# The experts' weights start 32 bytes further on in slots longer by 64 bytes, and one row tile is folded into another

## The chip, the cores and the metric

The kernel runs on one core of a Trainium2 chip. The metric is the device time of one execution, in microseconds (us). A time of the kernel is the median of several executions; the profile shows one execution on its own.

## The reference

Two model blocks are computed one after the other on x of 256 tokens by 1024 features, all in fp32. The first block has two layers of mLSTM and retention heads. The second has two layers of a mixer (a convolution beside banded attention), the first layer followed by a dense SwiGLU, the second by a mixture of eight experts of which each token uses two:

```
logits = t @ w_router + b_router
top_val, top_idx = lax.top_k(logits, 2)
combine = sum(one_hot(top_idx, 8) * softmax(top_val)[..., None], axis=1)
for e in range(8):
    out = out + combine[:, e:e + 1] * ((silu(t @ w_gate[e]) * (t @ w_up[e])) @ w_down[e])
```

Each expert has w_gate and w_up of 1024 x 3584 and w_down of 3584 x 1024. Every layer's shift, scale and gate come from a modulation `silu(c) @ w_ada[l] + b_ada[l]`.

## The kernel before

**Units.** All large weights stream once from HBM through one path, in units of 1 MB (128 partitions x 2048 fp32). SP's queue loads a unit into a slot of `raw` (`load`, L507). ScalarE casts it to the first part, `whi` (`high`, L707), VectorE subtracts to get the second part, `wlo = raw - whi` (`low`, L1738), and TensorE multiplies with both. A product of fp32 accuracy is made from three matmuls in TensorE's fp32r type: first part by first part, second by first, first by second. `whi` and `wlo` have HL = 3 slots of UW = 2048 elements (8192 bytes) in each partition; `raw` has 3 slots for weights before the experts and 6 in the experts. Semaphores tie the slots: SP waits for VectorE to have read a `raw` slot (raw_free), ScalarE and VectorE wait for TensorE to have used a `whi`/`wlo` slot (unit_done), TensorE waits for raw_free.

**The experts.** There are eight jobs of 42 units, 336 in all. 28 units hold columns of w_gate and w_up; for each of four row blocks in a unit there are three matmuls (L1641 to L1643) with a stationary operand of 128 x 128 tokens from `xghi` or `xglo`, and 512 columns of `whi` or `wlo` as the moving operand. 14 units hold rows of w_down; there `thi` and `tlo` are stationary (L1670 to L1672), and 512 columns of `whi` or `wlo` move again. That is 12 matmuls a unit. Between units there are short stretches of other matmuls: transposes (L1627), the spreading of a finished job (L1616), the gathering of tokens for the next (L1608).

**Before the experts** the weights are mostly the stationary operand, and 256 tokens of `hhi`, `hlo`, `yhi` or `ylo` move (L1127 to L1129, L1182 to L1184); for values they move, 256 columns at a time (L1168 to L1170). The gate products of the first block (L1336 to L1338) have `ghi` and `glo` as stationary operand, a narrow one of GROUP + H = 36 columns: slice d of these tiles starts 144·d bytes behind the tile's start, and there are eight slices with three matmuls each.

**Addresses.** Tiles lie one behind the other in the order in which they are allocated. In the built program `whi` starts at byte 65,664 of each partition, `wlo` at 90,240, `hhi` at 131,200, `thi` at 164,480, `xghi` at 201,344, `ghi` at 223,936 and `glo` at 225,088: all multiples of 64. All slots and all operands of 128 or more columns taken from them start at multiples of 64 as well.

**The modulation.** VectorE sums the products of `w_ada` units with the silu of c into `acc` and `acc2`, two running sums (`ada`, L1782 to L1797). In each mixer ScalarE copies a finished row from PSUM into `arow` (L1003), TensorE turns it into columns (L1541), and VectorE takes the columns.

Of the kernel before, what the change touches and what calls it, by code (L numbers as in the profile page):

```python
# [5 lines left out]
F32 = mybir.dt.float32  # L6
F32R = mybir.dt.float32r
I32 = mybir.dt.int32
ACT = mybir.ActivationFunctionType
ALU = mybir.AluOpType  # L10
AX = mybir.AxisListType

P = 128
S = 256
D = 1024
KD = D // P
# [22 lines left out]
FE = 3584  # L39
# [19 lines left out]

UW = 2048
RAW = 6
HALF = 3
MOE_SLOTS = (3, 4, 5, 2, 0, 1)
HL = 3
# [31 lines left out]
S_MOE = S_B3 + UNIT_L2  # L97
# [155 lines left out]
def two_block_model(nc, x, positions, consts, c, w_ada, b_ada, norm_g, w_in, conv_w, conv_b, b_igate, b_fgate,  # L253
# [7 lines left out]
    with ctx:  # L261
        def sb(name, shape, dt=F32, stack=ctx):
            return stack.enter_context(nc.sbuf_tensor(name, shape, dt))
# [3 lines left out]

        raw = sb("raw", [P, RAW, UW])
        whi = sb("whi", [P, HL, UW], F32R)  # L270
        wlo = sb("wlo", [P, HL, UW], F32R)
        xT = sb("xT", [P, KD, S])
        h = sb("h", [P, KD, S])
        hhi = sb("hhi", [P, KD, S], F32R)
# [17 lines left out]
        acc2 = sb("acc2", [P, S])  # L292
# [61 lines left out]
        b2 = ExitStack()  # L354
# [13 lines left out]
        st2 = sb("st2", [P, 2, 8], F32, b2)  # L368
        mean512 = sb("mean512", [P, P], F32, b2)
        cpad = sb("cpad", [P, KD, 2 * GROUP - 1], F32, b2)  # L370
        arow = sb("arow", [P, S], F32, b2)
        b2.close()

# [9 lines left out]
        thi = sb("thi", [P, FE // P, P], F32R, bm)  # L384
        tlo = sb("tlo", [P, FE // P, P], F32R, bm)
        htok = sb("htok", [P, 2, D], F32, bm)
        xghi = sb("xghi", [P, KD, 2, P], F32R, bm)
        xglo = sb("xglo", [P, KD, 2, P], F32R, bm)
# [40 lines left out]
        raw_free = sem("raw_free")  # L429
        hi_ready = sem("hi_ready")  # L430
# [269 lines left out]
        def _(act):  # L700
            step = Chain(act, scalar_step)

            def high(u):
                act.wait_ge(raw_in[u.raw], u.loads)
                if u.n >= HL or u.per:
                    act.wait_ge(unit_done, u.done(1 - HL))
                nc.scalar.copy(whi[:, u.hl, :], raw[:, u.raw, :]).then_inc(hi_ready, 1)  # L707

            def inverse_root(to, of, ready, value, least=eps, loaded=False):

# [51 lines left out]
            for l in range(L):  # L762
                for at, v in ((P1_BADA, b_ada[l]), (P1_NORM, norm_g[l]), (P1_CB, conv_b[l]), (P1_GNM, gn_m[l]), (P1_GNR, gn_r[l])):
                    k = v.shape[0] // P
# [44 lines left out]
            for l in range(L):  # L809
# [11 lines left out]
                for h_no in range(H):  # L821
                    hd = Head(l, h_no)
                    q, k, v, o, z, rq, rk, rv, rz = hd.units
# [197 lines left out]
            for j in range(FF_UNITS):  # L1021
                u, i = Unit(S_FF + j), j // 2
# [82 lines left out]
        def _(pe):  # L1105
            mm = nc.tensor.matmul
# [113 lines left out]
            for k in range(KD):  # L1220
                for t in range(2):
                    last = nc.tensor.transpose(ps2[k // 2][:, k % 2, t * P:(t + 1) * P], xtok[:, t, k * P:(k + 1) * P], ident)
# [4 lines left out]
            for i in range(L):  # L1227
                last = nc.tensor.transpose(ps4[4][:, i], prow[:, i, :], ident)
# [70 lines left out]
            for l in range(L):  # L1299
                if l:  # L1300
                    norm(l)
                for h_no in range(H):
                    hd = Head(l, h_no)
                    q, k, v, o, z, rq, rk, rv, rz = hd.units
# [27 lines left out]
                    else:  # L1332
                        pe.wait_ge(glo_ready, 2 * l + 2)
                        sums = ps2[6][0:GROUP + H, 0]
                        for d in range(KD):
                            mm(sums, ghi[:, d], hhi[:, d], start=d == 0, stop=False)  # L1336
                            mm(sums, ghi[:, d], hlo[:, d], start=False, stop=False)
                            last = mm(sums, glo[:, d], hhi[:, d], start=False, stop=d == KD - 1)  # L1338
# [4 lines left out]
                    if h_no == 0:  # L1343
                        pe.wait_ge(a_ready, l + 1)
                        for t in range(2):
                            last = mm(ps[5][:, t * H:(t + 1) * H], g_a[:, t * P:(t + 1) * P], ident[0:H, 0:H], start=True, stop=True)
# [22 lines left out]
                    if hd.n == 0:  # L1369
                        pe.wait_ge(rows_in, ROWS_LOADED)  # L1370
                        for i, rows in enumerate(P2_ROWS + (CW * CT, CW * CT)):
                            last = nc.tensor.transpose(ps4[6][:, i, 0:rows], prow[0:rows, L + i, :], ident[0:rows, 0:rows])
# [194 lines left out]
            for k in range(KD):  # L1567
# [3 lines left out]
                last = mm(ps[7][g:g + NE, 0:S], wr[:, k], h[:, k], start=k < 4, stop=k >= 4, skip_group_check=True)  # L1571
            last.then_inc(logits_done, 1)
            for i in range(4):
                for k in range(4 * (i % 2), 4 * (i % 2) + 4):
                    last = nc.tensor.transpose(ps[i][:, P * (k % 4):P * (k % 4) + P], h[:, k, i // 2 * P:(i // 2 + 1) * P], ident)
                last.then_inc(htok_done, 1)
                if i == 0:
                    pe.wait_ge(lrow_ready, 1)
                    for t in range(2):
                        last = mm(ps[7][:, S + t * NE:S + (t + 1) * NE], lrow[:, t * P:(t + 1) * P], sel[:, 0:NE], start=True, stop=True)  # L1580
# [38 lines left out]
            def expert(job, mine, x, following):  # L1619
                chunks = JOB_UP // 4  # L1620

                def turn(c):
                    pe.wait_ge(ma_ready, job.count(chunks, c + 1))
                    if c:
                        pe.wait_ge(tlo_ready, job.count(chunks, c))
                    for i in range(4):
                        last = nc.tensor.transpose(ps4[4][:, i], ma[:, c % 2, i * P:(i + 1) * P], ident)  # L1627
                    last.then_inc(turned, 1)

                for i in range(JOB_UP):  # L1630
                    u, c, kind, half = job.unit(i), i // 4, i % 4 // 2, i % 2
                    if c >= 2 and half == 0:
                        pe.wait_ge((mg_ready, ma_ready)[kind], job.count(chunks, c - 1))
                    if i < 2:
                        pe.wait_ge(xghi_ready, mine.whole(i))
                        pe.wait_ge(xglo_ready, mine.whole(i))
                    pe.wait_ge(raw_free, u.free())
                    o = ps[2 * kind + c % 2][:, :]
                    for kk in range(4):
                        k, w = 4 * half + kk, slice(512 * kk, 512 * kk + 512)  # L1640
                        mm(o, xghi[:, k, x], whi[:, u.hl, w], start=k == 0, stop=False)  # L1641
                        mm(o, xglo[:, k, x], whi[:, u.hl, w], start=False, stop=False)  # L1642
                        last = mm(o, xghi[:, k, x], wlo[:, u.hl, w], start=False, stop=k == KD - 1)  # L1643
                    last.then_inc(unit_done, 1)
                    if c and i % 4 == 1:
                        turn(c - 1)
                    if i % 4 == 3 and 1 <= c <= 4 and 1 <= job.n < NE:

                        if c == 1:
                            pe.wait_ge(yexp_ready, job.count(2, 0))  # L1650
                            pe.wait_ge(pickT_ready, job.count(1, 0))
                        else:
                            pe.wait_ge(spread_taken, job.count(4, c - 5))
                        spread(job, c - 1, ps2[7])
                    if i == 4 * 5 + 3:
                        if 1 <= job.n < NE:
                            pe.wait_ge(spread_taken, job.count(4, 0))
                        pe.wait_ge(pickw_ready, mine.count())
                        for t in range(2):
                            last = nc.tensor.transpose(ps[7][:, t * P:(t + 1) * P], pickw[:, t, x], ident)  # L1660
                        last.then_inc(pickT_done, 1)
                for d in range(JOB_DOWN):
                    u = job.unit(JOB_UP + d)
                    pe.wait_ge(tlo_ready, job.count(chunks, d // 2 + 1))
                    pe.wait_ge(raw_free, u.free())
                    for i in range(2):
                        f = 2 * d + i
                        for n in range(2):
                            o, w = ps[5 + n][:, :], slice(D * i + 512 * n, D * i + 512 * n + 512)
                            mm(o, thi[:, f], whi[:, u.hl, w], start=f == 0, stop=False)  # L1670
                            mm(o, tlo[:, f], whi[:, u.hl, w], start=False, stop=False)  # L1671
                            last = mm(o, thi[:, f], wlo[:, u.hl, w], start=False, stop=f == FE // P - 1)  # L1672
                    last.then_inc(unit_done, 1)
                    if d == 0:
                        turn(chunks - 1)
                    if following is not None and d % 3 == 1 and d < 12:
                        if d == 1:
                            pe.wait_ge(pick_ready, following.count())
                            pe.wait_ge(hthi_ready, 2)
                            pe.wait_ge(pickT_ready, job.count(1, 1))  # L1680
                        gather_pair(following, d // 3)
# [44 lines left out]
        def _(dve):  # L1726
            step = Chain(dve, vector_step)
            V = nc.vector
# [5 lines left out]
            def low(u):  # L1734
                dve.wait_ge(hi_ready, u.count())
                if u.n >= HL or u.per:
                    dve.wait_ge(unit_done, u.done(1 - HL))
                V.tensor_tensor(wlo[:, u.hl, :], raw[:, u.raw, :], whi[:, u.hl, :].bitcast(F32), ALU.subtract).then_inc(raw_free, 1)  # L1738

            def norm_tile(n, k):  # L1740
                V.scalar_tensor_tensor(h[:, k], xT[:, k], amul[:, n, k:k + 1], rstd[:], ALU.mult, ALU.mult).then_inc(t_ready, 1)
# [123 lines left out]
            for l in range(L):  # L1865

                last = V.tensor_scalar(par1[:, l, P1_GNM:P1_GNM + KD], par1[:, l, P1_GNM:P1_GNM + KD], 0.5, None, ALU.mult)
# [99 lines left out]
            for l in range(L):  # L1967
# [5 lines left out]
                for h_no in range(H):  # L1973
                    hd = Head(l, h_no)
                    q, k, v, o, z, rq, rk, rv, rz = hd.units
# [17 lines left out]
                    for tap in range(CONV_K):  # L1993
                        if h_no == 0 and tap == 2:
                            gates_summed(l)
                        for x in range(2):
                            for t in range(2):
                                w = column(l, h_no, P1_CW + tap * 2 * KD + x * KD, t)
                                src = qpad[:, x, t, tap:tap + S]
                                if tap == 0:  # L2000
                                    last = V.tensor_scalar(qacc[:, x, t], src, w, column(l, h_no, P1_CB + x * KD, t), ALU.mult, ALU.add)
                                else:
                                    step.wait(back=3)
                                    last = V.scalar_tensor_tensor(qacc[:, x, t], src, w, qacc[:, x, t], ALU.mult, ALU.add)
# [53 lines left out]
                    for o_, t in ((slice(0, S), S), (slice(S, S + P), P)):  # L2058
                        last = V.scalar_tensor_tensor(sT[:, o_], ps[2][:, o_], HD ** -0.5,
                                                      cst[:, h_no * S + C_DECAY:h_no * S + C_DECAY + t], ALU.mult, ALU.mult)  # L2060
# [209 lines left out]
            for j in range(FF_UNITS):  # L2270
                u, i = Unit(S_FF + j), j // 2
# [244 lines left out]
```

## Time and profile before

| | |
|---|---|
| median of 3 runs | 2150.38 us (2146.89 to 2151.61) |
| the profiled execution | 2151.25 us, of which 2149.4 us from the first to the last instruction |
| TensorE busy | 2096.3 us (98%) |
| VectorE busy | 1753.4 us (82%) |
| ScalarE busy | 1321.3 us (61%) |
| moved by DMA | 595.07 MB, mean 277 GB/s |
| the stretch of the experts | about 1150 to 2135 us of the span |

TensorE's busy time counts a matmul from its start to its modelled end, and the ends of matmuls lie behind the starts of the next ones. So how fast TensorE goes is read from the distance between starts in the timeline, not from the length of one matmul.

### The profile page before, as it was taken

The numbers are of one execution on the slowest core, as the hardware profiler recorded it, in microseconds if no ns is written. First come the engines' busy times: TensorE is split into PE (matmuls) and PEld (weight loads), VectorE is DVE, ScalarE is ACT, GpSimd is POOL, SyncE is SP. The second block draws the span as 40 slices with busy tenths as digits, with TensorE's granted clock in tenths as the row PEclk, the third lists the DMA queues.
The fourth block names the chain that finished last, engine by engine and source line by source line (L and its number), as shares of the span: only waits on it lengthen the run. The fifth ranks groups of instructions, "written<-read, shape, count | busy, mean of one in ns | idle before, by whom it ended". The sixth has DMA issues, their size and how long they took to land.

```text
span 2149.4 us, 33810 instructions
## 1 busy us (share of the span) xinstructions
PE 2096.3 (98%) x13585; PEld 1866.9 (87%) x13585; DVE 1753.4 (82%) x2161; ACT 1321.3 (61%) x1265; POOL 30.9 (1%) x60
## 2 busy tenths in 40 slices
PE   7999999999999999999999999999999999999998
PEld 5899999899999889999987888888888888888887
DVE  3978875877767878887877988888888888889887
ACT  3565554566645753434656777777777677776775
POOL 3000000000000000000000000000000000000000
PEclk8999999999999999999998999999999999999999
DMA  9777855666656548987545999999999999999995
GB/s 318 239 218 226 247 188 163 198 191 213 184 189 223 189 138 281 288 303 265 177 170 205 369 353 347 374 358 343 361 350 380 345 345 357 362 366 344 360 348 197
DMA packets 356161, 595.07 MB, mean 277 GB/s; under 512 B 10376, under 2 KB 201368, under 8 KB 356008
## 3 DMA queue, kind: packets, MB, share of 16 engines
q1 hardware_dynamic: 352864, 586.92, 79.1%
q0 software_dynamic: 2752, 5.86, 1.2%
q8 instruction: 110, 1.80, 0.3%
q14 instruction: 43, 0.35, 0.0%
q10 hardware_dynamic: 392, 0.13, 0.0%
HBM read 591.80 MB, written 4.22 MB: 277 GB/s over the span
## 4 chain that ended last, share of the span: by engine, by line
PE 82%; DVE 8%; DMA 3%; ACT 3%; issue 3%; SPq 0%; POOL 0%; DVEq 0%; POOLq 0%
PE ps L1641 9%; PE ps L1643 9%; PE ps L1642 9%; PE ps L1127 5%; PE ps L1128 5%; PE ps L1129 5%; PE ps L1670 5%; PE ps L1671 5%; PE ps L1672 5%; PE ps L1182 3%; PE ps L1183 3%; PE ps L1184 3%; DVE acc L1794 2%; DVE wlo L1738 2%; ACT whi L707 1%
## 5 line engine op out<-in xcount | busy, mean ns | idle before, releaser
L1738 DVE TENSOR_TENSOR wlo<-raw,whi 128x2048 fp32r<-128x2048 f32 x485 | 1109.0, 2288 | 264.9 <-ACT whi L707 249.5
L707 ACT CAST whi<-raw 128x2048 fp32r<-128x2048 f32 x485 | 926.0, 1909 | 389.0 <-PE ps L1643 133.7
L1127 PE MATMUL ps<-hhi,whi 128*128 128x256 f32 x1360 | 393.4, 289 | 0.2
L1128 PE MATMUL ps<-hlo,whi 128*128 128x256 f32 x1360 | 385.9, 284 | 0.0
L1129 PE MATMUL ps<-hhi,wlo 128*128 128x256 f32 x1360 | 385.8, 284 | 0.0
L1641 PE MATMUL ps<-whi,xghi 128*128 128x512 f32 x896 | 360.4, 402 | 0.8 <-DVE wlo L1738 0.8
L1643 PE MATMUL ps<-wlo,xghi 128*128 128x512 f32 x896 | 350.1, 391 | 0.0
L1642 PE MATMUL ps<-whi,xglo 128*128 128x512 f32 x896 | 349.0, 390 | 0.0
L1127 PEld LDWEIGHTS ps<-hhi,whi 128*128 128x128 f32 x1360 | 262.1, 193 | 7.3 <-issue 7.0
L1128 PEld LDWEIGHTS ps<-hlo,whi 128*128 128x128 f32 x1360 | 262.1, 193 | 0.3
L1129 PEld LDWEIGHTS ps<-hhi,wlo 128*128 128x128 f32 x1360 | 261.9, 193 | 0.0
L1643 PEld LDWEIGHTS ps<-wlo,xghi 128*128 128x128 f32 x896 | 168.2, 188 | 36.7
L1641 PEld LDWEIGHTS ps<-whi,xghi 128*128 128x128 f32 x896 | 168.3, 188 | 34.2 <-DVE wlo L1738 1.2
L1642 PEld LDWEIGHTS ps<-whi,xglo 128*128 128x128 f32 x896 | 168.6, 188 | 33.7
L1670 PE MATMUL ps<-whi,thi 128*128 128x512 f32 x448 | 175.3, 391 | 0.0
L1671 PE MATMUL ps<-whi,tlo 128*128 128x512 f32 x448 | 174.5, 390 | 0.0
L1672 PE MATMUL ps<-wlo,thi 128*128 128x512 f32 x448 | 174.4, 389 | 0.0
L1794 DVE SCALAR_TENSOR_TENSOR acc<-raw,cact,acc 128x256 f32<-128x256 f32 x324 | 132.7, 478 | 0.0
L1672 PEld LDWEIGHTS ps<-wlo,thi 128*128 128x128 f32 x448 | 84.1, 188 | 17.7
L1670 PEld LDWEIGHTS ps<-whi,thi 128*128 128x128 f32 x448 | 84.2, 188 | 16.8
L1671 PEld LDWEIGHTS ps<-whi,tlo 128*128 128x128 f32 x448 | 84.2, 188 | 16.6
L1168 PE MATMUL ps<-whi,hhi 128*128 128x256 f32 x320 | 92.3, 289 | 0.0
(398 smaller groups left out, 3029.8 us busy)
## 6 DMA issues: line engine op xcount, KB each, us to landing
raw<-in_moe_w_gate_dram SPq DMA_DIRECT2D x112, 1024.0 KB, 6.1
raw<-in_moe_w_up_dram SPq DMA_DIRECT2D x112, 1024.0 KB, 6.1
raw<-in_moe_w_down_dram SPq DMA_DIRECT2D x112, 1024.0 KB, 5.0
raw<-in_w_in_dram SPq DMA_DIRECT2D x92, 1024.0 KB, 5.6
raw<-in_w_ada_dram SPq DMA_DIRECT2D x69, 1024.0 KB, 7.8
raw<-in_w_out_dram SPq DMA_DIRECT2D x24, 1024.0 KB, 5.0
raw<-in_ffn_w_gate_dram SPq DMA_DIRECT2D x11, 1024.0 KB, 9.1
raw<-in_ffn_w_up_dram SPq DMA_DIRECT2D x11, 1024.0 KB, 8.3
```

The source lines that it names most:

```text
L707: nc.scalar.copy(whi[:, u.hl, :], raw[:, u.raw, :]).then_inc(hi_ready, 1)
L1127: mm(ps2[u.bank][:, j], whi[:, u.hl, w], hhi[:, k], start=k == 0, stop=False)
L1128: mm(ps2[u.bank][:, j], whi[:, u.hl, w], hlo[:, k], start=False, stop=False)
L1129: last = mm(ps2[u.bank][:, j], wlo[:, u.hl, w], hhi[:, k], start=False, stop=k == KD - 1)
L1641: mm(o, xghi[:, k, x], whi[:, u.hl, w], start=k == 0, stop=False)
L1642: mm(o, xglo[:, k, x], whi[:, u.hl, w], start=False, stop=False)
L1643: last = mm(o, xghi[:, k, x], wlo[:, u.hl, w], start=False, stop=k == KD - 1)
L1670: mm(o, thi[:, f], whi[:, u.hl, w], start=f == 0, stop=False)
L1671: mm(o, tlo[:, f], whi[:, u.hl, w], start=False, stop=False)
L1672: last = mm(o, thi[:, f], wlo[:, u.hl, w], start=False, stop=f == FE // P - 1)
L1738: V.tensor_tensor(wlo[:, u.hl, :], raw[:, u.raw, :], whi[:, u.hl, :].bitcast(F32), ALU.subtract).then_inc(raw_free, 1)
L1794: last = V.scalar_tensor_tensor(sums[k % 2], w[:, k], cact[:, block, k:k + 1], sums[k % 2], ALU.mult, ALU.add)
```

## The change

The two tiles of the parts are allocated with 16 more elements (64 bytes) in each slot, under new names. `whi` and `wlo` become views of their first 2048 elements, `ehi` and `elo` views that start 8 elements (32 bytes) further on. Units of the experts (`u.n >= S_MOE`) are cast into `ehi`, subtracted into `elo` and multiplied from there; all other units use `whi` and `wlo`. `arow` is no longer a tile of its own but another name of `acc2`.

```
+HALF_LINE = 8
...
-        whi = sb("whi", [P, HL, UW], F32R)
-        wlo = sb("wlo", [P, HL, UW], F32R)
+        wide_hi = sb("wide_hi", [P, HL, UW + 2 * HALF_LINE], F32R)
+        wide_lo = sb("wide_lo", [P, HL, UW + 2 * HALF_LINE], F32R)
+
+        whi, wlo = wide_hi[:, :, 0:UW], wide_lo[:, :, 0:UW]
+        ehi, elo = wide_hi[:, :, HALF_LINE:UW + HALF_LINE], wide_lo[:, :, HALF_LINE:UW + HALF_LINE]
...
-        arow = sb("arow", [P, S], F32, b2)
+        arow = acc2
...
-                nc.scalar.copy(whi[:, u.hl, :], raw[:, u.raw, :]).then_inc(hi_ready, 1)
+                nc.scalar.copy((whi if u.n < S_MOE else ehi)[:, u.hl, :], raw[:, u.raw, :]).then_inc(hi_ready, 1)
...
-                        mm(o, xghi[:, k, x], whi[:, u.hl, w], start=k == 0, stop=False)
-                        mm(o, xglo[:, k, x], whi[:, u.hl, w], start=False, stop=False)
-                        last = mm(o, xghi[:, k, x], wlo[:, u.hl, w], start=False, stop=k == KD - 1)
+                        mm(o, xghi[:, k, x], ehi[:, u.hl, w], start=k == 0, stop=False)
+                        mm(o, xglo[:, k, x], ehi[:, u.hl, w], start=False, stop=False)
+                        last = mm(o, xghi[:, k, x], elo[:, u.hl, w], start=False, stop=k == KD - 1)
...
-                            mm(o, thi[:, f], whi[:, u.hl, w], start=f == 0, stop=False)
-                            mm(o, tlo[:, f], whi[:, u.hl, w], start=False, stop=False)
-                            last = mm(o, thi[:, f], wlo[:, u.hl, w], start=False, stop=f == FE // P - 1)
+                            mm(o, thi[:, f], ehi[:, u.hl, w], start=f == 0, stop=False)
+                            mm(o, tlo[:, f], ehi[:, u.hl, w], start=False, stop=False)
+                            last = mm(o, thi[:, f], elo[:, u.hl, w], start=False, stop=f == FE // P - 1)
...
-                V.tensor_tensor(wlo[:, u.hl, :], raw[:, u.raw, :], whi[:, u.hl, :].bitcast(F32), ALU.subtract).then_inc(raw_free, 1)
+                hi, lo = (whi, wlo) if u.n < S_MOE else (ehi, elo)
+                V.tensor_tensor(lo[:, u.hl, :], raw[:, u.raw, :], hi[:, u.hl, :].bitcast(F32), ALU.subtract).then_inc(raw_free, 1)
```

No engine gets another instruction, another order or another wait. What changes are addresses. The tiles behind the two parts start 384 bytes (six slots of 64) further on: `hhi` at 131,584, `thi` at 164,864, `xghi` at 201,728, still multiples of 64. `wide_hi` starts at 65,664 and `wide_lo` at 90,432. The slots of `ehi` start at 65,696, 73,952 and 82,208, and those of `elo` at 90,464, 98,720 and 106,976: each is 32 bytes past a multiple of 64, and so is each moving operand of the experts' matmuls, while their stationary operands remain at multiples of 64.

## Rows read from the trace of the kernel before

**Rows 1.** The page: busy time of the engines, and TensorE's granted clock in 40 slices

```profile
PE 2096.3 (98%) x13585; PEld 1866.9 (87%) x13585; DVE 1753.4 (82%) x2161; ACT 1321.3 (61%) x1265; POOL 30.9 (1%) x60
...
PEclk8999999999999999999998999999999999999999
```

**Rows 2.** Windows: busy time of each engine, clock, DMA share and GB/s, experts

```profile
1150.00:2135.00 985.00, 982.81 (x4501) 813.91 (x4500) 860.85 (x542) 708.30 (x477) 0.00 (x0) 1.00 0.97 350
```

**Rows 3.** Lines L1642 and L1671: count, duration in ns (min/median/max), first and last start

```profile
L1642 PE MATMUL ps<-whi,xglo x896: 387/389/402, 1149.2 to 2097.8; 128*128 128x512 f32 x180
```
```profile
L1671 PE MATMUL ps<-whi,tlo x448: 387/389/398, 1229.6 to 2136.4; 128*128 128x512 f32 x150
```

**Rows 4.** Timeline of TensorE (start us, length us), in a unit of w_down

```profile
1504.13 0.39 PE L1670 MATMUL ps<-whi,thi 128*128 128x512 f32 x1
...
1506.17 0.39 PE L1670 MATMUL ps<-whi,thi 128*128 128x512 f32 x1
```

**Rows 5.** Timeline of TensorE, 24 matmuls of 256 columns apart

```profile
539.93 0.28 PE L1127 MATMUL ps<-hhi,whi 128*128 128x256 f32 x1
...
542.82 0.28 PE L1127 MATMUL ps<-hhi,whi 128*128 128x256 f32 x1
```

**Rows 6.** The chain, in order of time: four plain fp32 matmuls of 256 columns

```profile
1307.15 0.86 PE ps L1616 x4
```

**Rows 7.** Timeline of TensorE: gate products, first matmul of each slice, then L1168

```profile
53.98 0.28 PE L1336 MATMUL ps<-hhi,ghi 128*36 128x256 f32 x1
...
54.33 0.28 PE L1336 MATMUL ps<-hhi,ghi 128*36 128x256 f32 x1
...
54.69 0.28 PE L1336 MATMUL ps<-hhi,ghi 128*36 128x256 f32 x1
...
55.03 0.28 PE L1336 MATMUL ps<-hhi,ghi 128*36 128x256 f32 x1
...
55.39 0.28 PE L1336 MATMUL ps<-hhi,ghi 128*36 128x256 f32 x1
...
55.74 0.28 PE L1336 MATMUL ps<-hhi,ghi 128*36 128x256 f32 x1
...
56.09 0.28 PE L1336 MATMUL ps<-hhi,ghi 128*36 128x256 f32 x1
...
56.43 0.28 PE L1336 MATMUL ps<-hhi,ghi 128*36 128x256 f32 x1
...
56.77 0.28 PE L1168 MATMUL ps<-whi,hhi 128*128 128x256 f32 x1
```

**Rows 8.** Timeline of TensorE, units of w_gate behind a spreading (L1616)

```profile
1417.37 0.40 PE L1642 MATMUL ps<-whi,xglo 128*128 128x512 f32 x1
...
1419.22 0.39 PE L1641 MATMUL ps<-whi,xghi 128*128 128x512 f32 x1
...
1422.40 0.39 PE L1643 MATMUL ps<-wlo,xghi 128*128 128x512 f32 x1
```

**Rows 9.** Groups by line, 1300 to 2100 us: busy us, mean ns, idle before

```profile
L1738 DVE TENSOR_TENSOR wlo<-raw,whi 128x2048 fp32r<-128x2048 f32 x271 | 620.0, 2289 | 102.5 <-ACT whi L707 102.4
L707 ACT CAST whi<-raw 128x2048 fp32r<-128x2048 f32 x272 | 520.4, 1913 | 191.4 <-PE ps L1643 116.1 <-PE ps L1672 75.2
```

**Rows 10.** Waits of SP's queue, 1300 to 2100 us: us in total, times, longest

```profile
SPq L507 <- DVE wlo L1738: 638.8, 270, 3.2
```

**Rows 11.** DMA: rate from 1113 to 1130 us, then 1300 to 2100, then landings there

```profile
DMA packets 3195, 6.35 MB, mean 374 GB/s; under 512 B 108, under 2 KB 108, under 8 KB 3193
```
```profile
DMA packets 119871, 284.49 MB, mean 356 GB/s; under 512 B 4336, under 2 KB 4336, under 8 KB 119830
```
```profile
DMA to landing us min/median/max: 4.7/5.7/8.2
```

**Rows 12.** Tile arow: ScalarE's copy into it

```profile
L1003 ACT COPY arow<-ps x2: 372/372/373, 774.0 to 1108.4; 128x256 f32<-128x256 f32 x2
```

## Prediction

> **What bounds the kernel now.** The page comes first: TensorE is busy 98% of the span and its granted clock is full but for the start and the change of stage before the experts [rows 1]. Next the windows: in the 985 us of the experts TensorE is busy 982.81 us at a clock of 1.00, VectorE 860.85, ScalarE 708.30 [rows 2]. A busy TensorE may still be badly fed, so the third view is the waits. ScalarE's cast waits for TensorE to give a slot back, VectorE's subtraction waits for the cast [rows 9], and SP waits 638.8 us in 270 loads for a `raw` slot [rows 10]. Everybody waits backwards towards TensorE, so in this stretch its pace is the time. The DMA engines look full (share 0.97), but moved 350 GB/s [rows 2], against a mean of 374 GB/s over a stretch at 1113 us where several loads stood in the queue, its quiet last microsecond included [rows 11].
>
> The change moves exactly one thing that this could hang on: the place of the moving operand against a 64-byte grid, with the stationary operand left on the grid.
>
> **The change part by part.** The experts have 896 + 448 matmuls for each of three lines [rows 3], 3 x 1344 = 4032. At 0.2267 us that is 914 of the 985 us, and each nanosecond by which the distance changes is worth 4.03 us.
>
> What does 32 bytes do to the distance? No row shows a moving operand off the grid in fp32r. The nearest rows are the gate products, whose stationary operand walks over it: slice d starts 144·d bytes on, that is 0, 16, 32, 48, 0, 16, 32 and 48 bytes past a multiple of 64, under the same moving operands on the grid. The slices of three matmuls take 0.35, 0.36, 0.34, 0.36, 0.35, 0.35, 0.34 and 0.34 us [rows 7]. So 0.117 us each over the first six, and 0.113 over the last six matmuls, at 32 and 48 bytes. Against 0.1067 that is a surcharge of 6.7 ns, half of the usual one. These rows say that the surcharge is no constant, and that the two slices at 32 bytes are among the shortest; they don't prove the address, for slice 3 at 48 bytes took 0.36, the matmuls have only 36 stationary columns, and the pattern also settles with time. Such settling is seen elsewhere: behind a spreading eight matmuls take 1.85 us, 0.231 each, and the next fourteen 3.18 us, 0.227 each [rows 8]. So two streams, the moving one and the load of the next weights, fall into step with each other, and where each starts on the grid may set that step.
>
> Bounds. Best: the surcharge falls to the plain type's 1.7 ns; 11.7 ns x 4032 = 47 us less. Worst: every matmul keeps the distance of the unsettled ones, 0.231, or 4.6 ns more, +19 us; or it needs one 64-byte block more, 33 where there were 32, 16 columns at 2.4 GHz = 6.7 ns, +27 us. Between ends that far apart I take the nearest row, the 0.113 us of the slices at 32 and 48 bytes: the surcharge halves, 6.7 ns less a matmul, **6.7 x 4032 = 27 us less**.
>
> Does the rest keep pace? A unit falls from 985/336 = 2.93 us by 12 x 6.7 = 80 ns to 2.85. A unit is 1.0486 MB, so the loads need 368 GB/s, under the 374 of the loaded queue and with landings of 5.7 us, two units' time, in front of six slots [rows 11]. VectorE has 861 us of work for 958 us [rows 2], its subtraction is 2.289 us, the cast 1.913 [rows 9]. All this hides still; the cover is thin for the loads (at the best case of 2.79 us they need 376 GB/s, and a few us come back).
>
> The cast and the subtraction now write 32 bytes off the grid, and the subtraction reads one operand so. Between nothing and the whole slack: VectorE's idle time, 124 us over 336 units, is 0.37 us a unit, or 0.29 after the gain. I take nothing, since ScalarE and VectorE would have to lose a tenth of their rate before TensorE waited.
>
> `arow` as `acc2`: the same copy of 0.372 us, twice [rows 12]. It waits for the last sum as before, and VectorE's next sum stands behind its own wait for the turned row. Nothing, on either side of one copy (0.7 us in all). The 384 bytes by which the other tiles move leave the grid as it was; a grid of 128 bytes would be changed for the 256-column matmuls, since slots of 8256 bytes start alternately at 0 and 64 on it. Some seven thousand of them at 1 ns would be 7 us, of either sign; I take nothing.
>
> Sum: 2151.25 - 27 = **2124 us**. The profiled execution lies 0.9 us above the median of 2150.38, so against the median the same step gives 2123.5.
>
> The Trainium skill speaks against this sum. "TensorE: Matmul & The Clock Gate", section "Step-by-step: what each phase is for", gives the engine two independent read ports and says that loading the next weights takes no bandwidth from the running matmul. By that no address matters and the sum is 0. The same page's "Back-to-back issue gap" has 518 cycles for 512 columns; the trace's 0.2267 us are 544 cycles, so this case has a surcharge that the page doesn't know. "SBUF — State Buffer", section "Specifications (TRN2)", has lines of 16 bytes: 32 bytes are two whole lines, which again would change nothing.
>
> **The rivals.**
>
> 1. No effect. The surcharge could be a matter of time alone: it is 13.4 and 13.7 ns for operands of both widths, and the settling of [rows 8] happens with all addresses alike modulo 64. For it: slice 3. Against it: identical matmuls one after another settle within nine, the gate slices wander over eighteen. Time 2150.
> 2. Slower. If the moving stream is fetched in blocks of 64 bytes, 2048 bytes that begin half-way touch 33 blocks, and each matmul holds the stream for one block more: 6.7 ns, +27 us, 2178 us. It needs no conflict with the weights' load, only a fetch in rigid slots. It decides once the additional block costs more than the step regained: from +1.1 ns a matmul it is measurable. Against it: the gate slices at 32 and 48 bytes, which also straddle blocks, are on the mean no longer than those on the grid.
> 3. The surcharge vanishes: 2104 us, perhaps 2108 with the loads short of time.
> 4. A gain in a part only, since on a grid of 128 bytes the slots stand at 32 and 96 in turn: 1 to 5 ns on the mean, 2131 to 2147 us.
> 5. VectorE becomes the bound because of its shifted operands. It takes 13% more on its 2.289 us; nothing in the profile hints at it.
>
> **How the numbers follow.** The surcharge halves 0.38; vanishes 0.13; a part only 0.07: faster by more than 0.2% (about what a measurement of this kernel can tell from no change) 0.58. No effect 0.18. Slower 0.24: the additional block 0.19, rival 5 and the other tiles' 128-byte places 0.05. The likeliest case's own range is 2116 to 2132 (2 ns a matmul either way). The whole range goes from 2100, below case 3, to 2170, which takes in the unsettled distance of case 2 (2151 + 19) and leaves out its full block; that leaves out less than two tenths.
>
> **What the changed profile would show.** Right: in the timeline nine settled matmuls of the experts in 1.98 us in place of 2.04, the stretch of the experts about 958 us long, the 256-column matmuls before it still at 0.120, TensorE still without idle time, ScalarE's waits for TensorE shorter by some 80 ns a unit, DMA in the experts near 360 GB/s. No effect: 2.04 us again. The additional block: 2.10 us. VectorE as bound: a subtraction over 2.5 us, and TensorE idle behind L1738 (in the new numbering). The forecast is wrong if the step is set by time and not by address, or if the shift costs a block.

## The result

| | median | runs |
|---|---|---|
| before | 2149.58 us | 10 (2146.74 to 2151.81) |
| changed | 2156.93 us | 10 (2153.62 to 2160.83) |

The ratio is 1.0036, with a 95% interval of 1.0025 to 1.0046: the change makes the kernel slower by 0.36%. I had forecast 1.2% faster. The profiled execution took 2154.86 us, 2.1 us below its median, with a span of 2153.0 us; it is 3.6 us longer in its span than the profile before, and the comparison below accounts for these 3.6.

The page of the changed kernel, as in [rows 1]:

```profile
PE 2098.2 (97%) x13585; PEld 1850.4 (86%) x13585; DVE 1754.1 (81%) x2161; ACT 1318.9 (61%) x1265; POOL 31.0 (1%) x60
...
PEclk8999999999999999999999999999999999999999
```

The windows of the experts' stretch, as in [rows 2] (which had 985 us):

```profile
1134.00:2140.00 1006.00, 1004.61 (x4516) 816.96 (x4515) 863.11 (x544) 706.71 (x478) 0.00 (x0) 1.00 0.96 343
```

The experts' lines, as in [rows 3]. Every line has moved by 4 or 5 numbers:

```profile
L1646 PE MATMUL ps<-wide_hi,xglo x896: 389/393/403, 1134.7 to 2100.6; 128*128 128x512 f32 x180
```
```profile
L1675 PE MATMUL ps<-wide_hi,tlo x448: 389/393/403, 1216.6 to 2140.1; 128*128 128x512 f32 x150
```

From the first start of the one to the last of the other it is 1005.4 us, where [rows 3] give 2136.4 - 1149.2 = 987.2: the experts lost **18.2 us**. But their first matmul starts at 1134.7 instead of 1149.2: all that comes before them gained **14.5 us**. The sum is +3.7, the difference of the spans. Two effects of opposite sign, each more than three times the 0.2% (4.3 us) that the measurement can tell apart, nearly cancel.

Both are in the distance between starts. TensorE's timeline in a unit of w_down, two starts with 24 matmuls between them, then one of 256 columns before the experts, again 24 apart:

```profile
1375.70 0.39 PE L1674 MATMUL ps<-wide_hi,thi 128*128 128x512 f32 x1
...
1381.28 0.39 PE L1674 MATMUL ps<-wide_hi,thi 128*128 128x512 f32 x1
```
```profile
521.85 0.28 PE L1131 MATMUL ps<-hhi,wide_hi 128*128 128x256 f32 x1
...
524.67 0.28 PE L1131 MATMUL ps<-hhi,wide_hi 128*128 128x256 f32 x1
```

5.58 us for 24 is 0.2325 us, against 0.2267 in [rows 4]. 2.82 us for 24 is 0.1175, against 0.1204 in [rows 5].

The other engines have the same work as in [rows 9] and wait for TensorE a little longer, and SP's wait is that of [rows 10]:

```profile
L1743 DVE TENSOR_TENSOR wide_lo<-raw,wide_hi 128x2048 fp32r<-128x2048 f32 x266 | 608.9, 2290 | 115.0 <-ACT wide_hi L711 114.5
L711 ACT CAST wide_hi<-raw 128x2048 fp32r<-128x2048 f32 x267 | 508.7, 1905 | 200.1 <-PE ps L1647 119.4 <-PE ps L1676 80.7
```
```profile
SPq L511 <- DVE wide_lo L1743: 640.8, 265, 3.2
```

A subtraction takes 2.290 us (2.289 before), a cast 1.905 (1.913): places 32 bytes off the grid cost ScalarE and VectorE nothing.

In what follows, a job's mean distance is worked out from the starts of its 504 matmuls in the trace, those before which or behind which something else ran left out, as are the few stops of over 0.26 us. Before, it is 0.2277 to 0.2280 in the eight jobs; in the changed kernel 0.2326 to 0.2327. For the 256-column fp32r matmuls with the weights before the experts (7152, of which some 6900 have their like on both sides), it is 0.1199 before and 0.1176 changed. The short rows in fences show a stretch of 24, mostly settled, and can lie a nanosecond off their job's mean.

### The profile page after: what moved, and what is told of

Same layout as the page of the kernel before. It is cut to its first block, busy times and chain, and to the rows that moved or that the text cites. A ratio compares the mean times of both kernels' runs of the same rounds, so it can differ in the third digit from the quotient of the medians.

```text
span 2153.0 us, 33810 instructions
## 1 busy us (share of the span) xinstructions
PE 2098.2 (97%) x13585; PEld 1850.4 (86%) x13585; DVE 1754.1 (81%) x2161; ACT 1318.9 (61%) x1265; POOL 31.0 (1%) x60
## 4 chain that ended last, share of the span: by engine, by line
PE 85%; DVE 7%; issue 3%; ACT 3%; DMA 2%; SPq 0%; POOL 0%; DVEq 0%; POOLq 0%
PE ps L1647 9%; PE ps L1646 9%; PE ps L1645 9%; PE ps L1131 5%; PE ps L1132 5%; PE ps L1133 5%; PE ps L1676 5%; PE ps L1675 5%; PE ps L1674 5%; PE ps L1186 3%; PE ps L1187 3%; PE ps L1188 3%; DVE wide_lo L1743 1%; DVE acc L1799 1%; PE ps L1620 1%
## 5 line engine op out<-in xcount | busy, mean ns | idle before, releaser
L1743 DVE TENSOR_TENSOR wide_lo<-raw,wide_hi 128x2048 fp32r<-128x2048 f32 x485 | 1109.5, 2289 | 274.5 <-ACT wide_hi L711 257.9
L711 ACT CAST wide_hi<-raw 128x2048 fp32r<-128x2048 f32 x485 | 923.4, 1904 | 396.7 <-PE ps L1647 142.4
L1131 PE MATMUL ps<-hhi,wide_hi 128*128 128x256 f32 x1360 | 388.5, 286 | 0.4 <-DVE wide_lo L1743 0.4
L1132 PE MATMUL ps<-hlo,wide_hi 128*128 128x256 f32 x1360 | 380.5, 280 | 0.0
L1133 PE MATMUL ps<-hhi,wide_lo 128*128 128x256 f32 x1360 | 380.3, 280 | 0.0
L1645 PE MATMUL ps<-wide_hi,xghi 128*128 128x512 f32 x896 | 363.2, 405 | 0.6 <-DVE wide_lo L1743 0.6
L1647 PE MATMUL ps<-wide_lo,xghi 128*128 128x512 f32 x896 | 354.4, 395 | 0.0
L1646 PE MATMUL ps<-wide_hi,xglo 128*128 128x512 f32 x896 | 353.9, 395 | 0.0
L1131 PEld LDWEIGHTS ps<-hhi,wide_hi 128*128 128x128 f32 x1360 | 255.8, 188 | 7.4 <-issue 7.1
L1132 PEld LDWEIGHTS ps<-hlo,wide_hi 128*128 128x128 f32 x1360 | 256.8, 189 | 0.3
```

The lines of the kernel that those rows point to most:

```text
L711: nc.scalar.copy((whi if u.n < S_MOE else ehi)[:, u.hl, :], raw[:, u.raw, :]).then_inc(hi_ready, 1)
L1131: mm(ps2[u.bank][:, j], whi[:, u.hl, w], hhi[:, k], start=k == 0, stop=False)
L1132: mm(ps2[u.bank][:, j], whi[:, u.hl, w], hlo[:, k], start=False, stop=False)
L1133: last = mm(ps2[u.bank][:, j], wlo[:, u.hl, w], hhi[:, k], start=False, stop=k == KD - 1)
L1645: mm(o, xghi[:, k, x], ehi[:, u.hl, w], start=k == 0, stop=False)
L1646: mm(o, xglo[:, k, x], ehi[:, u.hl, w], start=False, stop=False)
```

## The experiments

Two theories stood at first. Theory A: the place of the moving operand on a grid of 64 bytes sets the pace, and the early gain has another source. Theory B: what counts is the distance in bytes between the places of the moving and the stationary operand, over a longer period; before the change all of them were alike modulo 512 bytes, and both the shift and the long slots ended that.

### The long slots alone

```
-        ehi, elo = wide_hi[:, :, HALF_LINE:UW + HALF_LINE], wide_lo[:, :, HALF_LINE:UW + HALF_LINE]
+        ehi, elo = whi, wlo
```

> The changed kernel with its slots longer by 64 bytes and arow in acc2, but the experts' weights at the slots' start (no shift of 32 bytes). The changed kernel's trace has the experts' matmuls at 0.2325 us each in place of 0.2267 and the 256-column fp32r matmuls before the experts at about 0.117 in place of 0.120. Theory A (only the place on a 64-byte grid counts for the experts, and something else, such as the 384 bytes by which the other tiles move, speeds the earlier part): experts back at 0.2267, earlier part as in the changed kernel, about 2133 us. Theory B (what counts is the place of moving and stationary operand to each other within some hundred bytes; before, all were equal modulo 512 bytes): the experts stay off their step, 0.229 to 0.233, the earlier part at 0.117, 2143 to 2157 us.

Measured: 2147.42 us, ratio 0.9997 (0.9988 to 1.0006). The two lines as above, and 24 matmuls of w_down:

```profile
L1646 PE MATMUL ps<-wide_hi,xglo x896: 387/393/398, 1133.6 to 2091.8; 128*128 128x512 f32 x180
```
```profile
L1675 PE MATMUL ps<-wide_hi,tlo x448: 388/393/398, 1214.9 to 2131.0; 128*128 128x512 f32 x150
```
```profile
1372.77 0.39 PE L1674 MATMUL ps<-wide_hi,thi 128*128 128x512 f32 x1
...
1378.28 0.40 PE L1674 MATMUL ps<-wide_hi,thi 128*128 128x512 f32 x1
```

The experts begin at 1133.6 (the early gain is whole) and take 997.4 us, ten more than before: 5.51 / 24 = 0.2296, job means 0.2305 to 0.2306. All operands are at multiples of 64 bytes here, so theory A can't explain these ten. In the medians the long slots alone are worth nothing that can be told from no change (2147.42 us, and 2149.20 for the kernel before, measured beside it), by a gain of 15 and a loss of 10; in the two profiles they are 5.0 us shorter.

### The shift alone

Both parts lie in one tile with slots of 8192 bytes; units of the experts start 32 bytes further on. All other tiles move by 512 bytes. Where the layouts meet, two casts wait for one unit more.

```
+        wide = sb("wide", [P, 2 * HL * UW + 128], F32R)
+
+        def part(k, n):
+
+            at = k * HL * UW + offset(n)
+            return wide[:, at:at + HL * UW].rearrange("p (s n) -> p s n", s=HL)
...
+                if u.n in (S_MOE, S_MOE + 1):
+                    act.wait_ge(unit_done, u.done(-1))
```

> Slots of 8192 bytes as before, all other tiles at their old places modulo 512, arow in acc2; only the experts' weights start 32 bytes further on. Both theories have the 256-column matmuls back at 0.120. Theory A: the experts at 0.2325, all of the loss of 24 us and none of the gain, 2173 us. Theory B: 0.229 to 0.235 according to what 32 bytes alone do, 2160 to 2180 us. If the experts stay at 0.2267 here, it was the slots' length alone: 2150 us.

Measured: 2175.95 us, ratio 1.0135 (1.0119 to 1.0150).

```profile
L1658 PE MATMUL ps<-wide,xglo x896: 389/394/397, 1151.8 to 2120.2; 128*128 128x512 f32 x180
```
```profile
L1687 PE MATMUL ps<-wide,tlo x448: 390/396/398, 1233.9 to 2159.9; 128*128 128x512 f32 x150
```
```profile
1393.42 0.40 PE L1686 MATMUL ps<-wide,thi 128*128 128x512 f32 x1
...
1399.03 0.40 PE L1686 MATMUL ps<-wide,thi 128*128 128x512 f32 x1
```

Nothing is gained before the experts (0.1199 a matmul; they start 2.6 us later than before, behind the two casts), and these take 1008.1 us: 5.61 / 24 = 0.2338, job means 0.2332 to 0.2333. That is 5.6 ns over the kernel before, 5.6 x 4032 = 22.6 us, against 20.9 measured in the stretch. The early part is as it was although `arow` is in `acc2`, so that plays no role, and neither does a move of all tiles behind the parts by 512 bytes. The early gain thus comes with the long slots. They bring two things at once that this run doesn't part: the slots' own starts, and the 384 bytes by which they push the tokens' tiles. The pairs further down show what the two make together.

### Sixteen distances

The same layout, with another distance in each job:

```
+OFFSETS = (0, 4, 8, 12, 16, 24, 32, 48)
...
+    return 0 if n < S_MOE else OFFSETS[min((n - S_MOE) // JOB_UNITS, NE - 1)]
```

> Slots of 8192 bytes as before; each of the eight jobs of the experts has its weights at another distance from the slots' start: 0, 16, 32, 48, 64, 96, 128 and 192 bytes. Read is the mean distance of the settled matmuls in each job. Theory A: 0.2267 at 0, 64, 128 and 192, higher at 16, 32, 48 and 96. Theory B: 0.2267 at 0 alone, every other distance has a value of its own, some of them perhaps under 0.2267. No effect of the place at all: 0.2267 in every job.

> As the other sweep, with distances of 0, 256, 320, 384, 448, 480, 8 and 0 bytes. Theory A: 0.2267 at 0, 256, 320, 384 and 448, higher at 480 and 8. Theory B: 0.2267 at 0 alone (jobs 0 and 7 alike), other values elsewhere. If 8 bytes already cost as much as 32, the line of 16 bytes is not what counts.

The numbers in `OFFSETS` are elements of 4 bytes. At each change of distance the first cast of a job waits for the whole job before it, so that the totals (2218.58 and 2214.66 us) say nothing; read are the jobs' means, in ns:

| bytes | 0 | 8 | 16 | 32 | 48 | 64 | 96 | 128 | 192 | 256 | 320 | 384 | 448 | 480 |
|---|---|---|---|---|---|---|---|---|---|---|---|---|---|---|
| mean | 227.7, 227.7, 227.8 | 233.7 | 231.6 | 233.3 | 233.3 | 231.1 | 233.3 | 232.5 | 233.3 | 227.9 | 230.6 | 232.6 | 233.3 | 233.2 |

The second run's jobs at 256 bytes and at 8 bytes, 24 matmuls each, and the first run's at 128:

```profile
1396.78 0.39 PE L1686 MATMUL ps<-wide,thi 128*128 128x512 f32 x1
...
1402.22 0.39 PE L1686 MATMUL ps<-wide,thi 128*128 128x512 f32 x1
...
2062.97 0.40 PE L1686 MATMUL ps<-wide,thi 128*128 128x512 f32 x1
...
2068.57 0.40 PE L1686 MATMUL ps<-wide,thi 128*128 128x512 f32 x1
```
```profile
2064.76 0.39 PE L1686 MATMUL ps<-wide,thi 128*128 128x512 f32 x1
...
2070.33 0.39 PE L1686 MATMUL ps<-wide,thi 128*128 128x512 f32 x1
```

5.44, 5.60 and 5.57 us. The pace at 256 is that at 0 (my expectation for theory B, 0 alone, was too narrow), and 64 and 320, 128 and 384, 192 and 448 agree within 0.6 ns: with both parts moved together the period is 256 bytes, or nearly so. Operands whose places are alike modulo 256 bytes are called level from here on. Theory A fails at 64, 128 and 192. Of all distances tried, the one that the kernel had is the best for the experts, and 8 bytes off it cost as much as 32.

### Long slots first, level ones for the experts

```
-        ehi, elo = wide_hi[:, :, HALF_LINE:UW + HALF_LINE], wide_lo[:, :, HALF_LINE:UW + HALF_LINE]
+        ehi, elo = (t[:].rearrange("p s n -> p (s n)")[:, at:at + HL * UW].rearrange("p (s n) -> p s n", s=HL) for t, at in ((wide_hi, 32), (wide_lo, 48)))
```

> The changed kernel's long slots for all units before the experts, and for the experts slots of 8192 bytes whose moving operands lie at the same place modulo 256 bytes as the stationary ones. So far: the experts take 0.2277 us a matmul at distances of 0 and 256 bytes, 0.2306 to 0.2337 at all others tried; the earlier part 0.1176 with long slots, 0.1199 without. Theory B (both are matters of the operands' places to each other, each part by itself) expects 0.2277 and 0.1176 together: 6950 x 2.3 ns = 16 us less than before, 2133 us. If something else in the long slots did it, or one part carries over to the other, the gain is under 8 us (over 2141 us).

Measured: 2144.13 us, ratio 0.9975 (0.9966 to 0.9984). Faster, by a third of the 16 us expected. The paces are as expected (0.1176, and job means of 0.2277 to 0.2280), and the experts take 987.1 us:

```profile
L1646 PE MATMUL ps<-wide_hi,xglo x896: 387/389/402, 1142.0 to 2090.6; 128*128 128x512 f32 x180
```
```profile
L1675 PE MATMUL ps<-wide_hi,tlo x448: 387/389/398, 1222.4 to 2129.1; 128*128 128x512 f32 x150
```

They start at 1142.0, though, not at 1134. ScalarE's timeline, casts of the experts' first two units, in the run with long slots alone and then in this one (in brackets, idle time before the cast and what ended it):

```profile
1101.66 1.91 ACT L711 CAST wide_hi<-raw 128x2048 fp32r<-128x2048 f32 x1
1107.76 1.91 ACT L711 CAST wide_hi<-raw 128x2048 fp32r<-128x2048 f32 x1 [2.89 <-PE ps L1188]
```
```profile
1104.45 1.91 ACT L711 CAST wide_hi<-raw 128x2048 fp32r<-128x2048 f32 x1
1116.09 1.90 ACT L711 CAST wide_hi<-raw 128x2048 fp32r<-128x2048 f32 x1 [8.44 <-PE ps L1188]
```

The second cast has to wait for the last unit of the mixer, not only for the last but one, because the new slot touches one still in use (this longer wait is not in the cut). That is 5.55 us more of idle ScalarE, with the norm's work queued behind it: the price of switching the layout, not of either layout. The other 2.8 of the 8.4 us had been lost before the first of these casts, and no run shows by what.

### Pairs of places

The two parts get separate places, in eleven stretches before the experts (the first number is the stretch's first unit, the others are elements of 4 bytes) and in the eight jobs:

```
+PLACES = ((0, 0, 16), (9, 0, 32), (18, 16, 32), (27, 16, 48), (44, 32, 48), ...
+JOB_PLACES = ((64, 128), (0, 16), (0, 32), (0, 48), (16, 64), (32, 64), (48, 64), (16, 32))
```

> Slots of 8192 bytes; the first and the second part of the weights each have a place of their own, in eleven stretches before the experts (distances of 0 to 256 bytes for the first, 64 to 448 for the second) and in eight jobs. Theory B expects another mean distance for each pair. If only one of the two parts counted, the jobs with the first part at 0 (second at 64, 128 and 192) would stay at 0.2277. In the earlier part the best single slot so far has 192 and 128 bytes modulo 256 (0.1161); the stretch with these places should show it.

> As the other run, with places that are multiples of 32 bytes. Its first stretch has both parts at 0 and must show 0.120. Theory B expects the odd multiples of 32 to be no worse on the mean than those of 64 in the earlier part, and all jobs but the first and the last to be above 0.2277.

> A third run with pairs of places, near the pair of 64 and 192 bytes in the earlier part, and eight new pairs in the experts. Theory B expects a value of its own for each pair, reproducible: the stretch with 64 and 192 bytes at 0.114 again, although it stands in another place of the program now (units 27 to 43 then as now, but with other pairs ahead), and the job with 256 and 512 bytes at 0.2277.

Totals (2219.94, 2218.82 and 2229.80 us) are again those of the stops. In the experts, first part level and second at 64, 128, 192 bytes: 232.1, 233.2 and 229.4 ns. So the second part, one matmul in three, counts as well. None of the twenty pairs other than level ones went below 229.1. The third run gave both parts 16 and then 128 bytes again, in other jobs than the sweep: 231.7 and 232.5 ns, against 231.6 and 232.5.

One job speaks against a plain rule modulo 256. With 64 bytes for the first part and 320 for the second, in the second run, the mean is 229.1 ns, where the sweep has 231.1 with both at 64 and 230.6 with both at 320. By such a rule these three are the same, and they lie further apart than repeated pairs do. Level parts show no such difference: 0 and 256 bytes, in the same run, gave 227.7. So which of the two parts lies 256 bytes further on can matter.

Before the experts, with the weights stationary, nearly all pairs lie between 116.3 and 119.7 ns, the level pair at 119.8. Multiples of 32 did no worse than those of 64. My guess for 192 and 128 bytes held about (116.4 in the first run and 116.2 in the second, with the second part at 384).

These pairs explain the early gain. In the changed kernel, and with the long slots alone, the three slots have the two parts 128 and 320, 192 and 384, 256 and 448 bytes past the place of the tokens' tiles, modulo 512. The changed kernel's means by slot are 118.3, 116.2 and 117.8 ns; the same pairs in these runs, with the tokens' tiles at another place, gave 118.4, 116.2 to 116.4, and 117.9.

One pair stands out: 64 and 192 bytes, in the first run and, behind other pairs, in the third; 24 matmuls each:

```profile
244.53 0.28 PE L1146 MATMUL ps<-hhi,wide 128*128 128x256 f32 x1
...
247.25 0.28 PE L1146 MATMUL ps<-hhi,wide 128*128 128x256 f32 x1
```
```profile
267.94 0.28 PE L1146 MATMUL ps<-hhi,wide 128*128 128x256 f32 x1
...
270.66 0.28 PE L1146 MATMUL ps<-hhi,wide 128*128 128x256 f32 x1
```

2.72 us, 0.1133 a matmul, and under 114 ns on the mean of some 700 matmuls in both runs. In the same units the matmuls in which the weights move took 117.7. For those the third run had a good pair of its own: 192 and 448 bytes, 113.6 ns on 93 matmuls, where the stationary ones took 117.6.

### That pair everywhere before the experts, level operands in them

No slot is longer. The tokens' tiles are moved, and the second part starts 128 bytes on, in the experts 256. At the switch two subtractions wait for one unit more than before (not in the cut):

```
+        wide_lo = sb("wide_lo", [P, HL * UW + 64], F32R)
+
+        wlo, elo = (wide_lo[:, at:at + HL * UW].rearrange("p (s n) -> p s n", s=HL) for at in (32, 64))
...
+        sb("gap", [P, 48])
         hhi = sb("hhi", [P, KD, S], F32R)
...
+        sb("gap_moe", [P, 16], F32, bm)
         thi = sb("thi", [P, FE // P, P], F32R, bm)
```

> Slots of 8192 bytes. Before the experts the first part lies 64 and the second 192 bytes past the place of the tokens' tiles, modulo 256 (a stretch of the pairs run with these places took 0.1139 us a matmul with the weights stationary and 0.1177 with them moving, against 0.1199 and 0.1199). In the experts both parts and the stationary tiles are at one place modulo 256. Theory B: 5600 matmuls x 6.0 ns + 1100 x 2.2 ns = 36 us less before the experts, and the experts at 0.2277 as before: 2113 us; up to 2125 if VectorE or the loads become late in the earlier part. If the stretch of the pairs run was fast for another reason (which head it was in), about 2135.

Measured: 2127.56 us, ratio **0.9901** (0.9885 to 0.9918), better than both kernels.

```profile
L1646 PE MATMUL ps<-whi,xglo x896: 387/389/398, 1125.7 to 2073.3; 128*128 128x512 f32 x180
```
```profile
L1675 PE MATMUL ps<-whi,tlo x448: 386/389/397, 1206.0 to 2111.9; 128*128 128x512 f32 x150
```
```profile
520.78 0.28 PE L1131 MATMUL ps<-hhi,whi 128*128 128x256 f32 x1
...
523.50 0.28 PE L1131 MATMUL ps<-hhi,whi 128*128 128x256 f32 x1
...
1362.09 0.39 PE L1674 MATMUL ps<-whi,thi 128*128 128x512 f32 x1
...
1367.53 0.39 PE L1674 MATMUL ps<-whi,thi 128*128 128x512 f32 x1
```

0.1133 and 0.2267, each as expected. The kernel before, measured beside it, had 2149.84 us. The experts start at 1125.7, 23.5 us earlier than before, and take 986.2 us. The 36 us were expected for a part in which TensorE sets the pace everywhere; the windows up to 380 us, of the kernel before and of this one, show that it doesn't:

```profile
0.00:380.00 380.00, 352.85 (x2747) 334.59 (x2748) 275.99 (x492) 198.67 (x248) 27.05 (x54) 0.96 0.74 230
```
```profile
0.00:380.00 380.00, 346.52 (x2748) 327.74 (x2749) 275.88 (x493) 198.69 (x248) 26.94 (x54) 0.95 0.74 231
```

In the first layer TensorE does the same work in 6 us less of busy time and stands idle in them; its longest wait there, for VectorE's tile `sT`, grew from 4.9 to 9.2 us in all. The gain begins behind that layer. It holds 44 of the 149 units before the experts, so by an estimate 44/149 of the 36 us, 11, had nowhere to go, and 25 were left, against 23.5 measured.

### Both operands off the grid

The shift alone once more, with the stationary tiles moved by the same 32 bytes:

```
+        sb("half_line", [P, 8], F32, bm)
         thi = sb("thi", [P, FE // P, P], F32R, bm)
```

> As the run with the shift alone, 32 bytes in the experts' weights, but their stationary tiles (thi, tlo, xghi, xglo) start 32 bytes further on too. If the experts' pace hangs on the place of the moving operand on a grid of 64 bytes (theory A) it stays at 0.233, 2176 us. If it hangs on the distance between moving and stationary operand (theory B) it is back at 0.2277, 2149 us.

Measured: 2154.22 us, ratio 1.0021 (1.0011 to 1.0030), and 24 matmuls:

```profile
1387.32 0.39 PE L1687 MATMUL ps<-wide,thi 128*128 128x512 f32 x1
...
1392.76 0.39 PE L1687 MATMUL ps<-wide,thi 128*128 128x512 f32 x1
```

5.44 us again, 0.2267, job means 0.2276 to 0.2280: theory B. The moving operands lie 32 bytes off the grid as in the kernel with the shift alone, and 22 us of loss are gone. The remaining 0.2% isn't in their pace. This kernel has the two casts with a longer wait at the switch of layouts: the first sits idle 6.37 us, against 0.17 in the kernel before, and in the profile the experts start 1.6 us later, which is the whole difference of the two spans. The medians differ by 4.4 us, and no run shows where the rest lies.

## Why the prediction was wrong

**What bounds the kernel** held. TensorE's pace is the time in the experts: the stretch grew by 18.2 us on 4032 matmuls, 4.5 ns each, and every other engine waited.

**The surcharge.** That there is one, fixed for each fp32r matmul and open to addresses, held too, and was more useful than the sum. It is 13.3 ns when all operands are level and 6.7 in the best pair before the experts, 113.3 ns.

**The step that failed** is the one from the gate products to the experts, "the surcharge halves", 27 us less. The measured term is +5.8 ns settled in the changed kernel and +6.7 with the shift alone. The 0.113 us of [rows 7] were real, but I took the slice's place on a grid of 64 bytes as their cause without a second row for it. The runs show that the distance between the two operands counts, for both parts, and that one pair of distances has different values where the weights stand still and where they move (under 114 and 117.7 ns). All of the experts' operands had been level, and no distance tried there is better. A row in which one thing varied among several gave a sign to a sum of 27 us. That slice 3 spoke against it, I wrote and then left out of the sum.

**The second step that failed** is "I take nothing" for the long slots in the earlier part. I priced "some seven thousand of them at 1 ns", of either sign, put it at 7 us, and gave it no case of its own, only a share of 0.05 on the slower side. It measured 2.3 ns, 14.5 us less. The price wasn't of the slots' place on a grid of 128 bytes either, but of the pairs of distances that they and the 384 bytes make. Had both terms been right, +18 and -15, the forecast would have been +4. That the measured 2156.93 us lies between my outer bounds of 2100 and 2170 is luck: two wrong terms of opposite sign.

**The rivals.** "No effect" fell: 8 bytes cost 6 ns. "Slower" named 2178 us and 2.10 us for nine matmuls; the shift alone measured 2175.95, and the changed kernel has 2.09 for nine. Its mechanism, one block more for operands that begin half-way, is refuted all the same, so the agreement is luck. With both operands off the grid every moving operand straddles and the pace is 0.2267, and at 64, 128 and 192 bytes nothing straddles and the pace is lost. What this rival had right is a size: with the shift alone the mean rises from 544 to 560 cycles, 16 more. The argument that I held against it was none: a gate slice of 144 bytes touches three blocks of 64 at each of its four places, so those at 32 and 48 bytes straddle no more than the others. "The surcharge vanishes" and "VectorE as the bound" didn't happen, and the last with a subtraction unchanged to a nanosecond. The gain "in a part only" was looked for on the experts' side, and stood on the other.

**The rule on the read ports.** By the Trainium skill, "TensorE: Matmul & The Clock Gate", section "Step-by-step: what each phase is for", the load of weights takes no bandwidth from the matmul. The traces don't agree for fp32r, as far as the pace goes: the matmuls' distance hangs on how both operands lie to each other, up to 6 ns in 227. Whether it is bandwidth that the load takes, no run shows. The Trainium skill's "SBUF — State Buffer", section "Specifications (TRN2)", has lines of 16 bytes. They don't show as such either: 16 and 32 bytes, whole lines, cost 3.9 and 5.6 ns.

**What stays open.** Why the pace comes back after 256 bytes, why 64 and 320 bytes are not 64 and 64, and why the values are what they are: the runs give the map, not the circuit. That two streams fall into step was argued from the settling and was tried only through addresses. The difference of the medians, 7.35 us, is larger than that of the profiles, 3.6; the profiled executions lie at different places in spreads of 5 and 7 us, and nothing here says more.

## What to carry to other kernels

Where the starts of fp32r matmuls are further apart than their columns explain, look at operand addresses: tabulate stationary minus moving modulo 512 bytes, and read the time between starts for each class. An address change acts on every user of the tile, so price the padding that makes room for it as well as the shift itself. Sweep before you choose: eight distances fit into one kernel when its work comes in like stretches, and one trace then gives all eight. The best places found here (64 and 192 bytes in one stage, level in the other) follow from no rule that the runs show.

## What the runs showed of the hardware

- fp32r matmuls with 128 stationary columns settle into times from start to start that depend on where moving and stationary operand lie to each other. With 512 columns these are 226.7 ns when all operands are level (alike modulo 256 bytes) and 229 to 234 on the mean at all other places tried. With 256 columns they are 120.0 when level and mostly 116 to 120 elsewhere; 64 and 192 bytes have 113.3 with the weights stationary, and 192 and 448 have 113.6 on the mean with the weights moving.
- Moved by 256 bytes together, both parts keep the pace within 0.6 ns. With the second part alone moved by 256 the pace changed by 2 ns in one case (229.1 against 231.1), and by nothing when both were level.
- The settled times when level, and the 113.3, are whole multiples of 16 cycles of 2.4 GHz: 544 (226.7 ns), 288 (120.0) and 272 (113.3). Plain fp32 matmuls keep to 0.215 to 0.216 us for 256 columns [rows 6], in every kernel here.
- As far as tried, only the distance counts, not the place: moved together by 32 bytes, level operands keep 226.7 ns, and three pairs of distances have the same means within 0.2 ns with the tokens' tiles at two places, 128 bytes apart modulo 256.
- For ScalarE's cast and VectorE's subtraction 32 bytes make no difference (1.905 and 2.290 us against 1.913 and 2.289).
